# One inference step of a two-layer hybrid trunk on one core: last expert pair's down matrices loaded in column halves, fetched rows of one tile added by the tensor engine, next norm tile by tile inside the pass, roots with scale and bias

## The chip, the core and the metric

The kernel runs on one core of one Trainium2 chip (trn2). The metric is the device time of one execution in microseconds (us), lower is better. The program is written engine by engine: TensorE (PE), VectorE (DVE), ScalarE (ACT), GpSimd (POOL), and the queues that only issue DMAs, SyncE (SP) above all. Each engine runs its own list in order, and waits on semaphores that others raise.

## What is computed

Two layers. Layer 0 mixes tokens with a gated linear recurrence, layer 1 with differential attention; each is followed by a hierarchical mixture of experts. There are 384 tokens (128 context, 256 latent), so three tiles of 128, and a width of 1024. All is float32. Cut to what matters here:

```
def rmsnorm(x, g):
    y = xf * lax.rsqrt(jnp.mean(xf * xf, axis=-1, keepdims=True) + EPS)
    return y * g
def hier_moe(u, ...):            # 4 groups of 4 experts, top-1 group, top-2 experts in it
    h = silu(einsum('nd,edf->nef', xt, w_gate)) * einsum('nd,edf->nef', xt, w_up)
    h = h * combine[:, :, None]                 # two weights per token, else zero
    y = einsum('nef,efd->nd', h, w_down)
# every sub-layer: x = x + gate * f(modulate(rmsnorm(x), shift, scale))
# layer 1 begins with q, k, v = split(modulate(rmsnorm(x)) @ w_qkv, 3)
```

## The kernel before

**The expert stage** (`experts(n)` on each engine, n is the layer) goes over 8 pairs of experts with `expert_passes`: `before`, eight times `body`, then `after`. If an expert had over 64 tokens, further passes would follow in a loop behind `If(count > 1)`; here one pass is enough, and each engine that reaches the end of its first pass loads the count, compares it and jumps over that loop. A pair has six weight matrices of 2 MB (gate and up of two experts, then down of two), which SP loads through a ring of eight slots; `expert_weights` waits until TensorE has used the slot. TensorE gathers the tokens of a pair by a one-hot product (L654), multiplies by gate and up (L665), turns the products (L718) and multiplies by down (`down`, L681) in two column halves of 512, which ACT copies out (L1163, L1166). For seven pairs ACT writes the results into a table in HBM (`expert_rows`).

**The end of the stage.** While the last pair is under way POOL (`collect`, L2023) fetches for every token its two result rows out of that table by six indirect DMAs, two for each tile, into `own` (which lies in `uT`) and into `second_rows` (ring slot 0 in layer 0). DVE (`after`, L1664 to L1669) weights the two rows, adds them and multiplies by the gate; POOL adds the sum to `x` (L2028). Tokens of the last pair do not go through the table: TensorE multiplies its results by the weighted one-hot `wc` (L741, three tiles, two halves), DVE gates that (L1676) and adds it to `x` (L1681), tile by tile, which raises `added`. Ahead of the last `down` TensorE does six products whose result nobody reads (`keep_busy`, L584).

**From layer 0 to layer 1.** ACT squares and sums `x` (L1059) and takes the root (L1063), between the two DVE divides by the width and adds EPS (`mean`, L1385); DVE takes the reciprocal and scales (`normalise`, L1391, L1392), TensorE turns each tile (`turn_tile`, L561, 8 transposes), ACT and DVE each modulate four of its eight feature blocks into `uT` (L1074, L1431), and TensorE starts the projection to q, k, v (L971, 18 blocks of 8 products). Before the turns stand eight more unread products (`keep_busy(8, 512)`). The same chain `square`, `mean`, `root`, `normalise` is used for the second norm of both layers (`second_square`, `second_norm`), for the head norm (`head_mean`, `head_root`), and for q and k in the projection.

**SP's order** at this place: the last pair's six matrices, then the six 2 MB blocks of `attn_w_qkv`, the first one (slot 1) as soon as the pair before last has used that slot.

## Time and profile before

| | |
|---|---|
| median of 3 runs | 1240.55 us (1237.82 to 1240.55) |
| profiled execution, its own time | 1240.84 us |
| its span, first to last instruction | 1239.0 us |
| busy: PE / DVE / ACT / POOL | 1141.3 / 428.6 / 225.6 / 136.1 us |
| DMA, mean over the span | 256 GB/s, 317 MB in all |
| mean granted TensorE clock | 0.976 of full |

The span is cut into 40 slices on the profile's page, with the busy share of each engine, the granted clock and the DMA rate. The timeline gives instructions in order of time, runs of the same kind merged: start, duration, engine, line, output<-inputs, count, and in brackets the idle time before and what ended it. A product of two float32 operands shows as two records, so "x12" is six products. POOL's row for an indirect DMA is the issue alone.

### The profile page before, as it was taken

The page shows a single profiled execution, that of the slowest core. Times are in us where ns is not written, and L with a number is a line of the kernel's source. Part 1 is how long each engine was busy: PE and PEld are TensorE (multiplying, and loading weights), DVE is VectorE, ACT ScalarE, POOL GpSimd, SP SyncE. Part 2 cuts the span into 40 slices and gives each one's busy share as a digit, 9 for nine tenths or more (in the row PEclk, how much of TensorE's full clock was granted, in tenths as well). Part 3 has the DMA queues.
Part 4 walks back from the last instruction along what each step waited for, and adds up shares of the span by engine and source line. Part 5 has one row for each costly group of instructions (what it writes and reads, how often), then busy time and mean ns, then how long its engine had stood idle before and what let it go on. Part 6 is the DMA issues. An engine that isn't in the chain of part 4 may idle for free.

```text
span 1239.0 us, 20044 instructions
## 1 busy us (share of the span) xinstructions
PE 1141.3 (92%) x8612; PEld 681.9 (55%) x8612; DVE 428.6 (35%) x1108; ACT 225.6 (18%) x523; POOL 136.1 (11%) x219
## 2 busy tenths in 40 slices
PE   4999999998899999999989899998989899999885
PEld 2566666665444576666654444444545756666552
DVE  2155555555522350100003755307853420000007
ACT  2210101011111321011000311116632221011010
POOL 0343433333100000000002100000000000000012
PEclk9999999999899999999989899998999999999998
DMA  9973444434923348999999913226751279999993
GB/s 337 316 242 110 138 138 137 137 137 176 380 103 125 136 163 335 424 426 426 424 426 409 346 68 115 106 100 237 262 235 64 73 295 426 426 425 426 424 423 143
DMA packets 97601, 317.08 MB, mean 256 GB/s; under 512 B 3792, under 2 KB 38912, under 8 KB 81120
## 3 DMA queue, kind: packets, MB, share of 16 engines
q1 hardware_dynamic: 90160, 298.05, 62.8%
q10 hardware_dynamic: 5248, 10.97, 2.3%
q0 software_dynamic: 2096, 6.67, 1.5%
q8 instruction: 72, 1.18, 0.4%
q14 instruction: 25, 0.20, 0.1%
HBM read 304.67 MB, written 11.01 MB: 255 GB/s over the span
## 4 chain that ended last, share of the span: by engine, by line
issue 70%; PE 20%; DVE 3%; DMA 3%; POOL 1%; ACT 0%; POOLq 0%; DVEq 0%
PE bank L775 10%; PE bank L784 4%; DMA ring<-expert_rows,moe_row 2%; PE bank L800 2%; PE bank L470 1%; DVE ring L1666 1%; DMA ring<-in_w_ada 1%; PE bank L856 1%; PE bank L809 0%; DVE hg_kf L1759 0%; PE bank L849 0%; DVE uT L1664 0%; PE bank L867 0%; PE bank L476 0%; DVE uT L1676 0%
## 5 line engine op out<-in xcount | busy, mean ns | idle before, releaser
L665 PE MATMUL bank<-ring,xn 128*64 128x256 f32 x1536 | 175.4, 387 | 10.7 <-DMA ring<-in_moe_w_up 7.9
L665 PEld LDWEIGHTS bank<-ring,xn 128*64 128x64 f32 x1536 | 112.1, 140 | 76.5 <-issue 12.8
L775 PE MATMUL bank<-uT,ring 128*128 128x384 f32 x384 | 135.0, 496 | 0.9 <-DVE uT L1712 0.9
L971 PE MATMUL bank<-ring,uT 128*128 128x512 f32 x288 | 126.6, 595 | 1.3 <-issue 1.3
L1654 DVE TENSOR_TENSOR moe_hh<-xn,bank 128x256 f32<-128x256 f32 x32 | 13.5, 421 | 308.0 <-ACT xn L1151 307.9
L2019 POOL TENSOR_TENSOR moe_flag<-con 128x1 f32<-128x1 f32 x2 | 0.4, 192 | 850.8 <-DMA expert_rows<-xn 850.8
L654 PE MATMUL bank<-moe_g,moe_h 128*128 128x128 f32 x768 | 92.2, 277 | 0.4 <-DVE moe_g L1552 0.4
L775 PEld LDWEIGHTS bank<-uT,ring 128*128 128x128 f32 x384 | 69.2, 190 | 42.1 <-issue 2.0
L654 PEld LDWEIGHTS bank<-moe_g,moe_h 128*128 128x128 f32 x768 | 88.2, 192 | 6.1 <-issue 6.1
L971 PEld LDWEIGHTS bank<-ring,uT 128*128 128x128 f32 x288 | 53.9, 191 | 65.4 <-issue 65.4
L681 PE MATMUL bank<-ring,xn 128*64 128x512 f32 x384 | 85.0, 595 | 0.6 <-DMA ring<-in_moe_w_down 0.6
L575 PE MATMUL bank<-ring,uT 128*128 128x512 f32 x192 | 84.0, 592 | 0.0
L1720 DVE COPY_PREDICATED hg_att<-masks,bank 128x384 f32<-128x384 uint8 x104 | 59.9, 576 | 0.0
L575 PEld LDWEIGHTS bank<-ring,uT 128*128 128x128 f32 x192 | 35.9, 190 | 42.2 <-issue 42.1
L665 PE MATMUL bank<-moe_ring,xn 128*64 128x256 f32 x512 | 57.2, 380 | 1.3 <-DMA moe_ring<-in_moe_w_up 1.3
L470 PE MATMUL bank<-ring,cT 128*32 128x512 f32 x384 | 53.8, 684 | 3.8 <-DMA ring<-in_w_ada 3.8
L681 PEld LDWEIGHTS bank<-ring,xn 128*64 128x64 f32 x384 | 27.4, 137 | 50.6 <-issue 49.5
L1151 ACT ACTIVATE xn<-bank 128x256 f32<-128x256 f32 x32 | 12.3, 383 | 206.4 <-PE bank L665 206.4
L665 PEld LDWEIGHTS bank<-moe_ring,xn 128*64 128x64 f32 x512 | 37.4, 137 | 22.1 <-issue 3.9
L784 PE MATMUL bank<-ring,uT 128*128 128x128 f32 x384 | 47.2, 277 | 0.0
L784 PEld LDWEIGHTS bank<-ring,uT 128*128 128x128 f32 x384 | 44.7, 192 | 0.6
L904 PE MATMUL bank<-ring,uT 128*128 128x512 f32 x96 | 42.2, 594 | 0.6 <-DVE adaln L1404 0.5
(269 smaller groups left out, 1306.2 us busy)
## 6 DMA issues: line engine op xcount, KB each, us to landing
ring<-in_w_ada SPq DMA_DIRECT2D x24, 2048.0 KB, 9.9
ring<-in_moe_w_gate SPq DMA_DIRECT2D x24, 2048.0 KB, 18.2
ring<-in_moe_w_up SPq DMA_DIRECT2D x24, 2048.0 KB, 22.4
ring<-in_moe_w_down SPq DMA_DIRECT2D x24, 2048.0 KB, 27.5
ring<-in_hgrn_w_in SPq DMA_DIRECT2D x32, 512.0 KB, 8.3
moe_ring<-in_moe_w_gate SPq DMA_DIRECT2D x8, 2048.0 KB, 22.5
moe_ring<-in_moe_w_up SPq DMA_DIRECT2D x8, 2048.0 KB, 24.1
moe_ring<-in_moe_w_down SPq DMA_DIRECT2D x8, 2048.0 KB, 21.1
```

The lines of the kernel that those rows point to most:

```text
L470: last = mm(bank[to][32 * g:32 * g + 32, :], cT[:, 2 * g + r, :], cols(slot)[:, 2 * g + r, :], start=(r == 0), stop=(r == 1))
L575: last = mm(bank[4 + half][:, :], uT[:, k, t * P:(t + 1) * P], cols(slot)[:, k, :], start=(k == 0), stop=(k == KC - 1))
L654: last = mm(bank[half][:, k * P:(k + 1) * P], m["h"][:, t, (4 * half + k) * P:(4 * half + k + 1) * P], m["g"][:, t, :, :], start=(t == 0), ...
L665: last = mm(bank[2 + e][64 * g:64 * g + 64, 256 * part:256 * part + 256], m["xe"][:, k, 64 * e:64 * e + 64], cols(slot)[:, k, 256 * g:256 ...
L681: last = mm(bank[5 + 2 * half][64 * e:64 * e + 64, :], m["hT"][:, e, j, 64 * g:64 * g + 64], rows_of[e][:, g, j, 512 * half:512 * half + 512],
L775: last = mm(to[:, 0:TOK], w[:, k, f, :], uT[:, k, :], start=(k == 0), stop=(k == KC - 1))
L784: last = mm(bank[3][:, t * P:(t + 1) * P], uT[:, k, t * P:(t + 1) * P], w[:, k, 1, :], start=(k == 0), stop=(k == KC - 1))
L800: last = mm(to[g * size:(g + 1) * size, here], lhs[:, here], rhs[:, here], start=True, stop=True)
L904: last = mm(bank[4 + half][:, :], uT[:, k, t * P:(t + 1) * P], cols(2 + half)[:, k, :], start=(k == 0), stop=(k == KC - 1))
L971: last = mm(bank[b % 2][:, :], uT[:, k, t * P:(t + 1) * P], cols(slot)[:, k, :], start=(k == 0), stop=(k == KC - 1))
L1654: v.tensor_tensor(m["hh"][:, e, :], m["sg"][:, e, :], bank[2 + e][:, 256:512], ALU.mult)\
L1720: return v.copy_predicated(HG["att"][:, :].rearrange("p (t n) -> p t n", t=T), mask, src[:, 0:TOK].rearrange("p (t n) -> p t n", t=T))
```

## The change

1. Last pair: the two down matrices are loaded as four DMAs of 512 columns each (`last_down`), first the left halves of both experts, then the right halves. The k order in the slot becomes (k p), and the turns of the last pair (L718 before) take adjacent columns to match. TensorE waits for the left halves alone (`down_half`), after two unread products instead of six.
2. TensorE's order for the last pair: down left half, the last pair's share of all three tiles for the left half (`first_halves`), down right half, the right half of tiles 0, 2 and 1, and then, for tile 1, four products by a diagonal of weights (`rw`, built by DVE from `ident`) that add its fetched rows in PSUM.
3. DVE's `after`: tile 0 complete, then the fetched rows of tile 2, then the norm of tile 0, tiles 1 and 2 in halves, norms of 1 and 2. POOL's three adds are gone.
4. Layer 0 alone: ACT squares and takes the roots inside the pass (`after` on ACT); TensorE turns tile 0 directly, without the eight unread products, and tiles 1 and 2 in the middle of the first two projection blocks. ACT modulates all of tile 0.
5. `mean` goes everywhere: the root takes scale 1/n and a bias column `eps`. `root_table` loads the root's table ahead at three places.
6. SP loads the first `attn_w_qkv` block when the last fetched rows have landed (`rows2`) instead of when slot 1 is free; the block of slot 0 waits for ACT's last root.

The core of the diff:

```
+                    if last:
+                        for part in range(4):
+                            expert_weights(n, i, part, p)
+                        last_down(n, p)
+                        return
...
+                for half in range(2):
+                    here = slice(512 * half, 512 * half + 512)
+                    for e in range(2):
...
+                        src = a["moe_w_down"][n, 2 * (PAIRS - 1) + e].rearrange("(k p) n -> p k n", p=P)
+                        sp.dma_start(down_rows(slot).rearrange("p g j n -> p (g j) n")[:, :, here], src[:, :, here])\
+                            .then_inc(S[n]["down_half"] if half == 0 else full[n][slot], 16)
...
-                sp.wait_ge(used[0][slot], count * USES + uses_before[0][slot])
-                if slot == SLOT_ORDER[0][0]:
-                    sp.wait_ge(S[0]["added"], count * T + (T - 1))
+                if b == 0:
+                    sp.wait_ge(S[0]["rows2"], count * 32)
...
-                        keep_busy(6, 512)
-                    rows_of = [down_rows(weights_in(i, 4 + e)) for e in range(2)]
+                        keep_busy(2, 512)
+                        pe.wait_ge(s["down_half"], at_pass[0] * 32 + 32)
...
+                        if half == 1 and i == PAIRS - 1:
+                            first_halves(it)
...
+                    last_pair(0, 1, True, True).then_inc(s["last_mm"], 1)
+                    last_pair(2, 1, True, True).then_inc(s["last_mm"], 1)
+                    last_pair(1, 1, True, False)
+                    pe.wait_ge(s["rows1"], p * 32 + 32)
+                    fetched_rows(0)
+                    fetched_rows(1).then_inc(s["last_mm"], 1)
...
-            keep_busy(8, 512)
-            for t, banks in enumerate(((6, 4), (2, 3), (5, 7))):
-                need(pe, 1, "xn_ready", t + 1)
-                turn_tile(1, "xT_done", xn, t, banks)
+            turn_features(0)
...
+                        if b < 2 and k == (6, 4)[b]:
+                            turn_features(b + 1)
...
+                    if n == 0:
+                        root_table()
+                        for t in range(T):
+                            act.wait_ge(s["added"], p * T + (T + t))
+                            A(second_rows[n][:, t, :], x[:, t, :], ACT.Square, accum_out=stat[:, 0, t:t + 1])\
+                                .then_inc(norm_act, 1)
+                            act.wait_ge(norm_act, p * (2 * T) + (2 * t + 1))
+                            root_of(stat[:, 2, t:t + 1], stat[:, 0, t:t + 1], D).then_inc(norm_act, 1)
...
+                    rows_summed(0)
+                    gated_rows(0)
+                    last_added(0, 0)
+                    last_added(0, 1)
+                    rows_summed(2)
+                    if n == 0:
+                        next_norm(0)
+                    for t in range(1, T):
+                        last_added(t, 0)
+                        last_added(t, 1)
+                    if n == 0:
+                        next_norm(1)
+                        next_norm(2)
...
-                    for t in range(T):
-                        pool.wait_ge(s["placed"], p * PLACED + (LAST_WEIGHTED + 3 * t + 3))
-                        g.tensor_tensor(x[:, t, :], x[:, t, :], second_rows[n][:, t, :], ALU.add).then_inc(s["row_added"], 1)
```

How TensorE's list reads from the turns of the last pair to the end of the pass, before (con is the constant tile of the unread products, moe_wc the weighted one-hot):

```order
L718 MATMUL bank<-con,moe_hh 128x128 x4
L584 MATMUL bank<-con 128x512 x6
L681 MATMUL bank<-ring,xn 64x512 x16
L741 MATMUL bank<-xn,moe_wc 128x512 x6
```

and with the change:

```order
L772 MATMUL bank<-con,moe_hh 128x128 x4
L609 MATMUL bank<-con 128x512 x2
L713 MATMUL bank<-ring,xn 64x512 x8
L724 MATMUL bank<-xn,moe_wc 128x512 x3
L713 MATMUL bank<-ring,xn 64x512 x8
L724 MATMUL bank<-xn,moe_wc 128x512 x3
L739 MATMUL bank<-uT,moe_rw 128x512
L739 MATMUL bank<-ring,moe_rw 128x512
L739 MATMUL bank<-uT,moe_rw 128x512
L739 MATMUL bank<-ring,moe_rw 128x512
```

Three of the six products of L741 moved between the halves of down; four products of L739 are new, at the end.

ACT's list from the last root to the first block of the projection, in the first pass of the change (L1241 is the square, L1122 the root; this is the end of the pass):

```order
L1241 ACTIVATE ring,stat<-x 128x1024
L1122 ACTIVATE stat<-stat,con 128x1
L334 TENSOR_LOAD npass
L334 ISA x2
L349 COMPARE_AND_BRANCH
L350 UNCONDITIONAL_BRANCH
```

and what it jumps to (L1137 modulates, L1371 is the first square of the projection):

```order
L1137 ACTIVATE uT<-bank,mod 128x128 x12
L1358 REGISTER_ALU
L1359 DMA at_v<-in_cache_v 128x1024
L1371 ACTIVATE xn<-bank 128x512
```

Before, the pass ended with L1166, and the squares and roots stood behind the jump. Now all three squares and roots stand ahead of it, and every modulation of tile 0, which the first projection block waits for, behind it.

TensorE's list where layer 1 begins, with the change (L586 turns a tile, L1028 is the projection, L1010 turns heads); before it was eight unread products, 24 turns, then 16 projection products without a break:

```order
L586 MATMUL bank<-con,xn 128x128 x8
L1028 MATMUL bank<-ring,uT 128x512 x7
L998 REGISTER_ALU
L586 MATMUL bank<-con,xn 128x128 x8
L1028 MATMUL bank<-ring,uT 128x512 x6
L998 REGISTER_ALU
L586 MATMUL bank<-con,xn 128x128 x8
L1028 MATMUL bank<-ring,uT 128x512 x3
L1010 MATMUL bank<-con,xn 128x128 x4
```

The turns of tiles 1 and 2 now stand inside the first two blocks.

## Rows read from the trace of the kernel before

**Rows 1.** Page, slices of 31 us, and busy time by engine in one stretch:

```profile
GB/s 337 316 242 110 138 138 137 137 137 176 380 103 125 136 163 335 424 426 426 424 426 409 346 68 115 106 100 237 262 235 64 73 295 426 426 425 426 424 423 143
480.00:560.00 80.00, 80.00 (x634) 51.58 (x632) 6.41 (x18) 9.14 (x18) 0.00 (x0) 1.00 1.01 425
...
L971 PE MATMUL bank<-ring,uT 128*128 128x512 f32 x288 | 126.6, 595 | 1.3 <-issue 1.3
```

**Rows 2.** DMA by queue (packets, MB, share), windows 672:675, 681:684 and 1200:1203:

```profile
q0 software_dynamic: 211, 0.77, 65.7%
q1 hardware_dynamic: 211, 0.43, 37.9%
...
DMA packets 568, 1.17 MB, mean 390 GB/s; under 512 B 7, under 2 KB 7, under 8 KB 566
...
DMA packets 170, 1.29 MB, mean 429 GB/s; under 512 B 13, under 2 KB 13, under 8 KB 13
```

**Rows 3.** Timeline of layer 0's last pair, PE and ACT:

```profile
659.11 3.67 PE L665 MATMUL bank<-ring,xn 128*64 128x256 f32 x32 [0.20 <-DMA ring<-in_moe_w_up]
...
665.23 5.42 PE L584 MATMUL bank<-con 128*128 128x512 f32 x12 [0.69 <-ACT xn L1157]
...
670.96 7.09 PE L681 MATMUL bank<-ring,xn 128*64 128x512 f32 x32 [0.32 <-DMA ring<-in_moe_w_down]
...
678.90 5.39 PE L741 MATMUL bank<-xn,moe_wc 128*128 128x512 f32 x12 [0.85 <-ACT xn L1166]
```

**Rows 4.** The same timeline, DVE's fetched rows, gates and adds:

```profile
672.09 0.75 DVE L1664 TENSOR_SCALAR uT<-uT,moe_hw 128x1024 f32<-128x1024 f32 x1 [8.35 <-DMA ring<-expert_rows,moe_row]
672.88 1.28 DVE L1666 SCALAR_TENSOR_TENSOR ring<-ring,moe_hw,uT 128x1024 f32<-128x1024 f32 x1
...
681.68 3.25 DVE L1666 SCALAR_TENSOR_TENSOR ring<-ring,moe_hw,uT 128x1024 f32<-128x1024 f32 x1
...
686.11 1.28 DVE L1676 TENSOR_TENSOR uT<-bank,gates 128x512 f32<-128x512 f32 x2
...
693.40 1.23 DVE L1681 TENSOR_TENSOR x<-x,uT 128x1024 f32<-128x1024 f32 x1
```

**Rows 5.** The same timeline, from layer 0's last product to the projection:

```profile
686.12 7.13 PE L584 MATMUL bank<-con 128*128 128x512 f32 x16 [1.84 <-issue]
...
692.20 1.06 ACT L1059 ACTIVATE moe_h<-x 128x1024 f32<-128x1024 f32 x1 [1.31 <-DVE x L1681]
...
694.89 0.17 DVE L1412 COPY mod<-adaln 128x16 f32<-128x16 f32 x1 [0.26 <-issue]
...
696.48 5.38 PE L561 MATMUL bank<-con,xn 128*128 128x128 f32 x24 [3.22 <-DVE xn L1392]
...
697.69 3.15 ACT L1074 ACTIVATE uT<-bank,mod 128x128 f32<-128x128 f32 x8
...
701.65 2.67 PE L971 MATMUL bank<-ring,uT 128*128 128x512 f32 x5
```

**Rows 6.** Windows: PE, PEld, DVE, ACT, POOL busy, granted clock, DMA share, GB/s:

```profile
696.00:702.00 6.00, 5.52 (x25) 5.51 (x26) 5.05 (x15) 4.74 (x14) 0.00 (x0) 0.50 1.05 391
702.00:704.00 2.00, 2.00 (x5) 0.76 (x4) 1.81 (x7) 0.55 (x2) 0.00 (x0) 0.91 1.06 389
...
1207.00:1211.00 4.00, 4.00 (x7) 1.53 (x6) 0.00 (x0) 0.00 (x0) 0.48 (x1) 0.57 1.02 409
```

**Rows 7.** Timeline of layer 1's last pair and the end:

```profile
1206.62 7.11 PE L584 MATMUL bank<-con 128*128 128x512 f32 x12 [0.69 <-ACT xn L1157]
...
1213.66 7.09 PE L681 MATMUL bank<-ring,xn 128*64 128x512 f32 x32
...
1233.61 1.22 DVE L1681 TENSOR_TENSOR x<-x,uT 128x1024 f32<-128x1024 f32 x1
```

**Rows 8.** Timeline of the second norm of tile 2 in layer 0:

```profile
426.90 0.15 DVE L1385 TENSOR_SCALAR stat<-stat 128x1 f32<-128x1 f32 x1 [1.21 <-ACT xn L1059]
...
428.33 1.09 PE L561 MATMUL bank<-con,xn 128*128 128x128 f32 x8 [0.96 <-DVE xn L1392]
```

More of the change, by code:

```diff
@@ L395, in expert_weights @@
                     sp.wait_ge(*free)
+                    if i == 0 and part == 0 and not isinstance(p, int):
+                        if n == 0:
+                            sp.wait_ge(norm_act, p * (2 * T))
+                        else:
+                            sp.wait_ge(S[n]["added"], p * T + (T - 1))
                 elif n == 0:
@@ L1669, in after @@
[L1669 to L1681 removed]
+                        await_step(step(v.tensor_scalar(own_row, own_row, m["hw"][:, 0, t:t + 1], None, ALU.mult)))
@@ L1693, in _ @@
             own(v.tensor_copy(bias_col[:, :], bank[4][:, 32:128]))
-            for t in range(T):
-                mean(0, "squares", "mean_ready", t)
             for t in range(T):
```

235 lines of the change are left out of this document (135 added, 100 removed).

## The prediction

> **What bounds the kernel now.** I read the page's slices first. In the expert stages the DMA rate stands at 424 to 426 GB/s, and TensorE is busy for all of 480 to 560 us [rows 1]: weights and products go side by side, and the DMA sets the pace. Nothing in the change touches that part. It touches the seams: the end of both expert stages, and the start of layer 1. So I read the timeline there. In layer 0 the last gate and up product waits for its matrix until 659.11, the unread products start at 665.23, and down waits for its matrices until 670.96; 7.09 us of down, a copy and 5.39 us of L741 end at 684.3 [rows 3]. From there the chain is DVE's and ACT's: gates and adds from 686.11 to 694.63 [rows 4], then square, root, scale, turns and modulation until the projection starts at 701.65 [rows 5]. The projection itself is TensorE's own: 126.6 us busy, 1.3 us idle [rows 1]. In layer 1 the unread products start at 1206.62, down at 1213.66, and DVE's last add ends at 1234.83; the output and the end of the span, 1239.0, follow 4.2 us behind [rows 7].
>
> **The last down matrices, layer 0.** The four new DMAs carry the same 4.19 MB. Three things change. (a) Packets. A row of 512 float32 is 2 KB, as in the projection's blocks, which run at 390 GB/s where the wide ones run at 429 [rows 2]. (b) The fetched rows compete. While both queues are at work, queue 0 (the rows) and queue 1 move equal numbers of packets, 211 each in 3 us, so queue 1 with its 2 KB packets gets 0.43 MB (143 GB/s) and the rows with 4 KB packets 0.77 MB (257 GB/s) [rows 2]. Wide packets had the better of that; narrow ones do not. (c) The first projection block no longer stands behind them.
> Estimate: the down bytes begin at about 656 (3 us ahead of the landing at 659.11, rows 3) and the rows reach the DMA engines at 665.3. Until then 9.3 x 0.386 MB, less 0.25 MB of other writes, is 3.35 MB; the last 0.84 MB at 143 GB/s take 5.9 us, and with 3 us to the semaphore they land at 674.2. The left halves land before 665.
> TensorE: two unread products, 5.42/6 each, from 665.23 to 667.0; the left half of down (7.09/2) to 670.6; 0.85 for the copy; three products of 0.90 (5.39/6) to 674.1; the right half, just landed, to 677.7; a copy again to 678.5; three products and the four new ones, 6.3 us, to 684.8 [rows 3]. Before, the end was 684.3. The down product starts 4 us earlier and nothing is won: four new products (3.6 us) and a second wait for the copy (0.85) take it.
> A rule of the Trainium skill speaks against this edit: DMA: Bandwidth & Descriptors, section Bandwidth, wants DMAs of 1 MiB and more and measures 341 GB/s at that size against 425 at 16 MB. No row here shows a 1 MB load of this kind by itself; by that rate the estimate for the landing would be 3 us later in each layer.
>
> **DVE after it.** Gone are POOL's three adds, beside which a 1.28 us operation took 3.25 [rows 4]. Tile 0 is gated, added and normed while TensorE works, so it costs nothing as long as that cover holds (it needs the rows by about 679; the first ones landed at 672.09, rows 4). Behind the last product, at 684.8, stand two gate-add pairs for tile 1 and two triples for tile 2: ten half-tile operations at 0.64 (L1676, half of 1.28) plus the gap, say 0.70 each: 691.8, against 694.63. That is 2.8 us won.
>
> **From x to the projection.** ACT's square, read and root of tile 2 cost 1.06 + 0.19 + 0.2, to 693.4. Now what the lists show: ACT's modulation of tile 0 stands behind all three squares and the jump out of the pass. Tile 0 is turned at 688, and nobody modulates it until tile 2's root is out. The jump: TensorE's shows 1.84 us before the next instruction, DVE's 0.26, hidden under a long add [rows 5]. ACT's root takes 0.2 and hides little, so I take 1.3, ends 0.3 and 1.9. Four modulations (half of 3.15) follow [rows 5]: the projection starts at 696.3, 5.3 us earlier.
> Then what is given back. The clock: before, TensorE was idle for 3.2 us, and 696 to 702 ran at 0.50, that is 1.2 GHz instead of 2.4 [rows 5, 6]; it came back about 5.9 us after work resumed, 0.7 us into the projection, and the low stretch had fallen on 24 short turns. Now the eight unread products are gone, TensorE idles from 688 to 696.3, and the low stretch falls on full products: 5.7 us at half speed lose 2.85, against 0.35. The turns of tiles 1 and 2 move into the projection: 16 at full clock, 1.09 per 8 [rows 8], 2.1 us, and 0.4 of waiting for their modulation. So the saving is 5.3 - 2.5 - 2.1 - 0.4 = **0.3 us**, ends -3 (a landing late by 3 us) and +4 (no jump to pay, the clock back early).
> The projection's blocks: the first is requested at about 677.5 and there by 686; the others take 5.4 us each and are needed every 21. Free. The 12 steps of `mean` taken out of the projection's chain are worth 0: TensorE covers them. If that cover were gone, 12 x 0.2.
>
> **The end, layer 1.** The unread products start at 1206.62, and the clock was low from 1207 to 1211 [rows 6, 7]. Two of them and the left half therefore end at about 1213.8, the copy at 1214.6, three products at 1217.3; the right halves, by the working above 2 us slower than before the change, land at about 1216.5. Right half to 1220.9, copy, seven products: 1228.0. Ten DVE operations: 1235.0 to 1235.4, against 1234.83. The output behind it is the same. Cost: **0.4 us**, ends -1.5 and +4.
>
> **Roots.** In the second norm of tile 2 TensorE waits for the chain, 0.96 us, and `mean` is 0.19 of it (from 426.90 to the root) [rows 8]: 0.2 us in each layer, **0.4 us** saved. With the expert stage bound by DMA it is kept only since SP's loads wait for slots that TensorE frees. The table loads are moved from places where they wait beside TensorE's work: 0, save 0.1 at the head norm of layer 1, which its own table load ahead gives back. The first norm of layer 0 lies under the wait for `w_ada`: 0.
>
> **Sum.** -0.3 + 0.4 - 0.4 = -0.3 us on the profiled time of 1240.84, that is 1240.5; the median of the runs lies 0.3 below that execution, so 1240.3.
>
> **The rivals.**
> *Forecast: an even exchange.* 1240.3 within 0.3% (3.7 us, about what a measurement of this kernel tells from no change). Chance 0.58.
> *Faster: the projection's early start is kept.* TensorE's clock does not stay low for long once full products come (4.4 us after work resumed in layer 1, rows 6, 7), ACT pays no jump, and the end of layer 1 gains from landing early. 1.5 (clock) + 1.0 (jump) + 1.5 (layer 1) + 1 (turns hidden in gaps): 1235.5. For it: the jump of DVE at 0.26. Against: an idle time of 3.2 us was enough to lower the clock before, and now it is 8. Chance 0.26.
> *Slower: the right halves land late.* The one mechanism is the equal split by packets: whatever of the 2.1 MB of right halves is still to come when the fetched rows start goes at 143 GB/s. The point of decision is a landing behind 674.1 in layer 0 and 1217.3 in layer 1, from there each us counts once in each layer. If all of the right halves were left, they would take 14.7 us and land about 7 us late. Likely is 3 us in each layer, 1246.5. For it: the split is measured. Against: most bytes should be through by 665. Chance 0.13. The rule on DMA size above would give this result too.
> *It does not do what it says.* The left halves are not early, because four DMAs on the same 16 engines finish together: then TensorE waits until 671 for its left half and ends 4 us late, 1244.5 to 1248. Chance 0.03.
>
> **How the numbers follow.** Faster by over 3.7 us: 0.26. Within: 0.58. Slower: 0.16. The range 1235.5 to 1245.5 takes in the forecast with its ends, most of the faster case and the milder half of the slower one.
>
> **What would show it.** Down's left half starting near 667 and 1209, its right half near 674 and 1217; the last product by `rw` ending near 684.8; DVE's last add of layer 0 near 692; ACT's first modulation 1 to 2 us behind the last root; the first projection product near 696, with a granted clock of 0.5 in the 5 us after it. I am wrong if the right half of down waits for its DMA, if the clock is full when the projection starts, or if anything between 705 and 1200 changes its length.

## The result, and the profile after

| | before | after |
|---|---|---|
| median, runs on the same chip | 1239.02 us (9 runs) | 1245.56 us (9 runs) |
| ratio | | 1.0054, 95% interval 1.0040 to 1.0068 |
| profiled execution / its span | 1240.84 / 1239.0 us | 1247.2 / 1245.4 us |
| busy PE / DVE / ACT / POOL | 1141.3 / 428.6 / 225.6 / 136.1 us | 1129.4 / 412.2 / 230.0 / 120.4 us |

The change makes the kernel 6.5 us slower. The forecast was an exchange, 1240.3 us; the measured time lies just above the range, and it is the time of the rival on the slower side, "the right halves land late" (1246.5 us). TensorE, DVE and POOL are less busy than before (ACT 4 us more): the loss is waiting.

TensorE's timeline of the changed kernel, end of layer 0 and start of layer 1, which answers to [rows 3] and [rows 5] (start us, duration, engine, line, output<-inputs, count, idle time before):

```profile
655.79 3.67 PE L690 MATMUL bank<-ring,xn 128*64 128x256 f32 x32 [1.34 <-DMA ring<-in_moe_w_up]
...
661.82 1.98 PE L609 MATMUL bank<-con 128*128 128x512 f32 x4 [0.69 <-ACT xn L1221]
663.74 3.65 PE L713 MATMUL bank<-ring,xn 128*64 128x512 f32 x16
668.18 2.81 PE L724 MATMUL bank<-xn,moe_wc 128*128 128x512 f32 x6 [0.79 <-ACT xn L1227]
674.22 6.55 PE L713 MATMUL bank<-ring,xn 128*64 128x512 f32 x16 [3.23 <-DMA ring<-in_moe_w_down]
681.54 2.84 PE L724 MATMUL bank<-xn,moe_wc 128*128 128x512 f32 x6 [0.77 <-ACT xn L1230]
...
686.80 1.02 PE L739 MATMUL bank<-ring,moe_rw 128*128 128x512 f32 x2
688.91 1.09 PE L586 MATMUL bank<-con,xn 128*128 128x128 f32 x8 [1.09 <-issue]
698.87 8.79 PE L1028 MATMUL bank<-ring,uT 128*128 128x512 f32 x14 [8.87 <-ACT uT L1137]
```

L713 is down, L724 the last pair's share, L739 the products by `rw`, L1028 the projection. The left half starts at 663.74 without a wait, 8.0 us behind the start of the last up product (655.79); before, down started 11.9 us behind it. Then the right half waits 3.23 us for its DMA, and takes 6.55 us where the left one took 3.65. The last product ends at 687.8, 32.0 us behind that same point; before, it was 25.2 [rows 3].

The DMA queues of the changed kernel in three stretches of 3 us (packets, MB, share of the 16 engines' time), first 661 to 664:

```profile
q0 software_dynamic: 207, 0.78, 66.5%
q1 hardware_dynamic: 207, 0.41, 36.1%
```

667 to 670:

```profile
q0 software_dynamic: 268, 0.99, 83.5%
q1 hardware_dynamic: 113, 0.22, 19.0%
```

670 to 673:

```profile
q0 software_dynamic: 139, 0.48, 39.6%
q1 hardware_dynamic: 41, 0.08, 6.7%
```

Queue 0 carries the fetched rows, queue 1 the right halves. At first they move equal numbers of packets, 207 each, as in [rows 2]. Later queue 1 gets less than half, and at the end 41 packets in 3 us: both queues together move 0.56 MB there (187 GB/s), and TensorE waits. Queue 1's last packets move between 673 and 674.

The granted clock of the changed kernel in those stretches (columns: stretch, length, busy PE, PEld, DVE, ACT, POOL, clock, DMA share, GB/s):

```profile
672.00:676.00 4.00, 1.78 (x6) 0.64 (x8) 0.93 (x2) 0.00 (x0) 0.00 (x0) 0.66 0.29 70
676.00:680.00 4.00, 4.00 (x12) 1.27 (x10) 0.00 (x0) 0.00 (x0) 0.00 (x0) 0.50 1.04 402
680.00:684.00 4.00, 3.23 (x10) 1.25 (x7) 1.26 (x2) 2.08 (x3) 0.00 (x0) 0.99 1.06 389
...
700.00:704.00 4.00, 4.00 (x6) 1.55 (x5) 0.00 (x0) 0.13 (x1) 0.00 (x0) 0.50 1.05 385
704.00:708.00 4.00, 4.00 (x14) 1.97 (x13) 0.00 (x0) 0.00 (x0) 0.00 (x0) 1.00 0.99 365
```

While TensorE waits for the right half the clock falls to 0.50 of full, that is 1.2 GHz for 2.4, and the right half is multiplied at that. It falls again in the 8.87 us without work before the projection, and comes back behind 704.

DVE's timeline of the changed kernel, which answers to [rows 4]:

```profile
666.92 0.75 DVE L1748 TENSOR_SCALAR uT<-uT,moe_hw 128x1024 f32<-128x1024 f32 x1 [6.50 <-DMA ring<-expert_rows,moe_row]
...
682.71 0.69 DVE L1765 TENSOR_TENSOR ring<-bank,gates 128x512 f32<-128x512 f32 x1 [9.74 <-PE bank L724]
...
687.86 0.69 DVE L1765 TENSOR_TENSOR ring<-bank,gates 128x512 f32<-128x512 f32 x1 [0.76 <-PE bank L739]
...
694.01 0.69 DVE L1766 TENSOR_TENSOR x<-x,ring 128x512 f32<-128x512 f32 x1
```

And ACT's, behind the last addition:

```profile
694.74 1.06 ACT L1241 ACTIVATE ring<-x 128x1024 f32<-128x1024 f32 x1 [2.62 <-DVE x L1766]
...
695.92 0.29 ACT L1122 ACTIVATE stat<-stat,con 128x1 f32<-128x1 f32 x1
697.22 2.90 ACT L1137 ACTIVATE uT<-bank,mod 128x128 f32<-128x128 f32 x8 [1.01 <-issue]
```

DVE waits 9.74 us for TensorE in the middle, and 6.8 us of additions follow the last product. ACT starts the modulation of tile 0 only at 697.22, 1.01 us behind the last root.

The end of layer 1, TensorE and then DVE, which answers to [rows 7]:

```profile
1203.74 3.67 PE L690 MATMUL bank<-moe_ring,xn 128*64 128x256 f32 x32 [1.67 <-DMA moe_ring<-in_moe_w_up]
...
1211.69 3.65 PE L713 MATMUL bank<-ring,xn 128*64 128x512 f32 x16
...
1222.07 5.35 PE L713 MATMUL bank<-ring,xn 128*64 128x512 f32 x16 [3.12 <-DMA ring<-in_moe_w_down]
```

```profile
1234.55 0.69 DVE L1765 TENSOR_TENSOR ring<-bank,gates 128x512 f32<-128x512 f32 x1 [1.82 <-PE bank L739]
...
1240.71 0.69 DVE L1766 TENSOR_TENSOR x<-x,ring 128x512 f32<-128x512 f32 x1
```

The right half waits 3.12 us here too. From the start of the last up product to the end of DVE's last addition it is 37.7 us; before 34.7.

To see where time goes, I cut each trace at seven points: the first gate product of layer 0, the last up product of layer 0, the projection's first product, the first scores of the attention, the same two points in layer 1, and DVE's last addition. The stretches from gate to last up product are 212.8 to 213.1 us long in both layers of every trace but one, where the last up product of layer 0 shows no gap of its own. The others (us, from start to start; the last column runs to the end of the addition):

| trace | start to first gate product | last up to projection | projection to scores | scores to layer 1's experts | last up, layer 1, to last addition |
|---|---|---|---|---|---|
| before | 446.0 | 42.5 | 134.4 | 151.1 | 34.7 |
| after | 442.8 | 43.1 | 139.0 | 152.9 | 37.7 |
| before, second trace | 444.6 | (255.8 from the first gate product; before 255.6) | 134.4 | 151.1 | 34.7 |
| after, second trace | 446.1 | 41.7 | 138.3 | 150.3 | 36.0 |
| rows held | 442.6 | 36.9 | 138.7 | 153.6 | 32.8 |
| gap filled | 444.3 | 40.2 | 139.1 | 151.3 | 36.0 |
| projection filled (8) | 444.5 | 41.7 | 138.2 | 152.7 | 37.6 |
| whole matrices | 443.9 | 44.1 | 138.8 | 152.6 | 39.3 |
| no products by rw | 444.9 | 41.0 | 139.0 | 152.9 | 36.0 |
| held and filled | 443.4 | 38.5 | 136.4 | 153.6 | 32.8 |
| the same, whole matrices | 443.4 | 40.9 | 136.4 | 151.7 | 34.8 |
| the same, order swapped | 445.3 | 36.9 | 136.5 | 152.7 | 31.0 |
| the same, turn outside | 445.1 | 40.5 | 134.9 | 151.7 | 32.8 |
| the last two together | 444.3 | 40.5 | 134.9 | 150.3 | 31.0 |

The first and the fourth column differ by 3.3 and 2.6 us between the two traces of the changed kernel alone, so they say nothing of an edit of a few us. In the fourth it goes with the clock: what the granted clock lacked of full, summed over slices of 5 us, is 5.1 us in the two traces of 150.3 us, 6.8 in the four of 151.1 to 151.7 (the kernel before twice among them), 8.5 to 8.6 in the five of 151.7 to 152.9, and 10.2 to 10.3 in the three of 152.6 to 153.6. The other three columns are what the experiments are read by. (Rows held is experiment 1 below, gap filled 2, projection filled 3, whole matrices 4, held and filled 6, no products by rw 7, and the last four rows are 8 to 11.)

### The profile page after: what moved, and what is told of

Same layout as the page of the kernel before. It is cut to its first block, busy times and chain, and to the rows that moved or that the text cites. A ratio compares the mean times of both kernels' runs of the same rounds, so it can differ in the third digit from the quotient of the medians.

```text
span 1245.4 us, 19994 instructions
## 1 busy us (share of the span) xinstructions
PE 1129.4 (91%) x8596; PEld 673.9 (54%) x8596; DVE 412.2 (33%) x1087; ACT 230.0 (18%) x530; POOL 120.4 (10%) x213
## 4 chain that ended last, share of the span: by engine, by line
PE 73%; DMA 12%; DVE 5%; ACT 2%; SPq 2%; issue 2%; ACTq 0%; DVEq 0%
PE bank L690 13%; PE bank L1028 10%; PE bank L829 10%; PE bank L600 7%; PE bank L713 7%; DMA ring<-in_moe_w_up 6%; PE bank L679 5%; DMA ring<-in_moe_w_down 5%; PE bank L838 4%; PE bank L958 3%; PE bank L495 3%; SPq L428 2%; DMA ring<-in_w_ada 2%; PE bank L854 2%; PE bank L579 1%
## 5 line engine op out<-in xcount | busy, mean ns | idle before, releaser
L690 PE MATMUL bank<-ring,xn 128*64 128x256 f32 x1536 | 172.6, 383 | 10.2 <-DMA ring<-in_moe_w_up 7.4
L1028 PE MATMUL bank<-ring,uT 128*128 128x512 f32 x288 | 129.5, 604 | 10.5 <-ACT uT L1137 9.2
L713 PE MATMUL bank<-ring,xn 128*64 128x512 f32 x384 | 90.1, 622 | 8.5 <-DMA ring<-in_moe_w_down 8.5
L1028 PEld LDWEIGHTS bank<-ring,uT 128*128 128x128 f32 x288 | 54.3, 193 | 75.5 <-issue 74.4
L600 PE MATMUL bank<-ring,uT 128*128 128x512 f32 x192 | 84.0, 593 | 0.0
L713 PEld LDWEIGHTS bank<-ring,xn 128*64 128x64 f32 x384 | 28.8, 142 | 61.8 <-issue 60.8
L495 PE MATMUL bank<-ring,cT 128*32 128x512 f32 x384 | 51.0, 653 | 5.8 <-DMA ring<-in_w_ada 5.8
L1215 ACT ACTIVATE xn<-bank 128x256 f32<-128x256 f32 x32 | 12.3, 384 | 204.4 <-PE bank L690 196.2
L958 PE MATMUL bank<-ring,uT 128*128 128x512 f32 x96 | 42.2, 594 | 0.6 <-DVE adaln L1473 0.5
```

The lines of the kernel that those rows point to most:

```text
L495: last = mm(bank[to][32 * g:32 * g + 32, :], cT[:, 2 * g + r, :], cols(slot)[:, 2 * g + r, :], start=(r == 0), stop=(r == 1))
L600: last = mm(bank[4 + half][:, :], uT[:, k, t * P:(t + 1) * P], cols(slot)[:, k, :], start=(k == 0), stop=(k == KC - 1))
L690: last = mm(bank[2 + e][64 * g:64 * g + 64, 256 * part:256 * part + 256], m["xe"][:, k, 64 * e:64 * e + 64], cols(slot)[:, k, 256 * g:256 ...
L713: last = mm(bank[5 + 2 * half][64 * e:64 * e + 64, :], m["hT"][:, e, j, 64 * g:64 * g + 64], rows_of[e][:, g, j, 512 * half:512 * half + 512],
L958: last = mm(bank[4 + half][:, :], uT[:, k, t * P:(t + 1) * P], cols(2 + half)[:, k, :], start=(k == 0), stop=(k == KC - 1))
L1028: last = mm(bank[b % 2][:, :], uT[:, k, t * P:(t + 1) * P], cols(slot)[:, k, :], start=(k == 0), stop=(k == KC - 1))
```

## The experiments

Three theories were weighed. A: the right halves share the DMA engines with the fetched rows and land late, and the wait lowers the clock. B: the order itself costs, with its four products by `rw` and its second copy, whenever the data lands. C: the loss is in layer 1's start, from clock, turns and ACT's order. The first four ran together on one chip (kernel before: 1237.77 us), the next four on another occasion (1238.02), the last four on a third (1238.21); each ratio is to the kernel before beside it.

**1. Hold the fetched rows back until the left halves have landed.**

```
@@ collect, POOL
+                    pool.wait_ge(s["down_half"], p * 32 + 32)
                     g.tensor_tensor(m["flag"][:, 1:2], ones[:, 0:1], ones[:, 0:1], ALU.mult)
```

> The changed kernel with one wait more: POOL starts the fetch of rows only when the left halves of the last down matrices have landed. Theory A (the fetched rows on queue 0 and the right halves on queue 1 share the DMA engines packet by packet, the right halves land 3.2 us late in layer 0 and 3.1 us late in layer 1, and each wait lowers TensorE's clock): the right half of down starts without a DMA wait in both layers, takes 3.7 us in place of 6.55 and 5.35, and the last product ends about 5.5 us earlier in layer 0 and 4.5 us earlier in layer 1. Of the 5.5 in layer 0 about 1 us can be lost where the rows now land later than the products by them want them. Total 8 to 10 us less than the changed kernel: 1235 to 1238. Theory B (the four products by the fetched rows, the second copy and the order of products cost the time, whenever the halves land): under 3 us less, 1243 or more. Theory C (the loss lies in layer 1's start, clock and turns inside the projection): the gain of layer 0 is kept as far as DVE's adds follow the products.

Measured: 1237.59 us, ratio 1.0004 (0.9987 to 1.0021). TensorE's timeline:

```profile
655.61 3.67 PE L690 MATMUL bank<-ring,xn 128*64 128x256 f32 x32 [1.22 <-DMA ring<-in_moe_w_up]
...
667.99 2.81 PE L724 MATMUL bank<-xn,moe_wc 128*128 128x512 f32 x6 [0.79 <-ACT xn L1227]
670.74 3.65 PE L713 MATMUL bank<-ring,xn 128*64 128x512 f32 x16
...
680.43 1.02 PE L739 MATMUL bank<-ring,moe_rw 128*128 128x512 f32 x2
...
692.49 8.52 PE L1028 MATMUL bank<-ring,uT 128*128 128x512 f32 x14 [9.57 <-ACT uT L1137]
```

Queues of this kernel, 660 to 663, 663 to 666, 666 to 669:

```profile
q1 hardware_dynamic: 545, 1.08, 97.5%
```

```profile
q0 software_dynamic: 59, 0.24, 32.9%
q1 hardware_dynamic: 142, 0.27, 23.1%
```

```profile
q0 software_dynamic: 257, 0.95, 91.8%
```

Alone, queue 1 moves its 2 KB packets at 387 GB/s (586 packets, 1.16 MB, from 657 to 660) and at 360 in the next 3 us, and is through by 666, before TensorE asks at 670.7. The right half waits for nothing and takes 3.65 us. The projection starts 6.2 us earlier after the last up product than in the changed kernel, the last addition of layer 1 4.9 us earlier. The rows arrive 2.9 us later than in the changed kernel (DVE's first operation on them at 669.66 in place of 666.92, with nearly the same up product), and nobody waits for them behind that. Theory A holds, and B falls as the main cause: the same order of products, without the late landing, is even with the kernel before. The three stretches of this one trace add up to 3.3 us less than before, while the medians are even and the interval allows 1.6 us less. In its fourth column it is 2.5 us longer than the kernel before; how much of the gain in the stretches an average execution keeps stays open.

**2. Keep TensorE busy while the right half is awaited.**

```
@@ down, TensorE
                             first_halves(it)
+                            fill(1, 3)
                             for e in range(2):
                                 weights_in(i, 4 + e)
```

(`fill(to, times)` is `keep_busy` with the bank as an argument.)

> The changed kernel with three unread products of 512 columns (0.95 us each) between the three products of the left half and the wait for the right half, into a bank that nobody reads. Theory A with the clock as a cost of its own: the right halves land as late as before, but TensorE stays at full clock, so the right half takes 3.7 us in place of 6.55 in layer 0 and 5.35 in layer 1: 3 to 4.5 us less than the changed kernel, 1241 to 1242.5. If the low clock after the wait has another cause, or if the time is given back behind it, nothing: 1245.5.

Measured: 1243.29 us, ratio 1.0046 (1.0028 to 1.0063).

```profile
672.29 2.74 PE L614 MATMUL bank<-con 128*128 128x512 f32 x6
675.68 3.65 PE L719 MATMUL bank<-ring,xn 128*64 128x512 f32 x16 [0.65 <-DMA ring<-in_moe_w_down]
```

The landing stays where it was, 18.4 and 18.3 us behind the last up product, but the clock holds and the right half takes 3.65 us in both layers. So the wait and the clock are two costs: 3.2 us and up to 2.9 us in layer 0, 3.1 and up to 1.7 in layer 1. (The 2.9 stands in one trace. In the three other traces with a late landing and nothing in the gap the clock cost 1.5 to 1.7 us, but nothing in layer 1 of the second trace in experiment 5.) By the ratios the clock's part is 1 to 3.6 us, against the two runs of the changed kernel (1.0054, and 1.0075 in experiment 5); the three intervals overlap, so it rests on the trace.

**3. Keep TensorE busy before the projection, eight products.**

```
@@ before the projection, TensorE
             turn_features(0)
+            fill(1, 8)
```

> The changed kernel with eight unread products of 512 columns (0.95 us each, 7.6 us) between the turn of tile 0 and the projection of layer 1, where TensorE is idle for 8.9 us. Theory C: the first 14 records of the projection take 6.2 us in place of 8.79 and the attention stage starts 2.6 us earlier: 1243. If the fill runs past the first modulation (it starts 7 to 8 us behind the turn), up to 1 us of it is lost. If ACT or the turns pace the first blocks, nothing: 1245.5.

Measured: 1243.51 us, ratio 1.0043 (1.0024 to 1.0061).

```profile
690.04 7.03 PE L614 MATMUL bank<-con 128*128 128x512 f32 x16
699.13 7.94 PE L1034 MATMUL bank<-ring,uT 128*128 128x512 f32 x14 [2.06 <-ACT uT L1143]
```

A miss: the 14 records take 7.94 us, not 6.2. The fill ended 2.06 us before the first modulated blocks were there, and the clock fell again: 0.86 from 698 to 700, 0.50 from 700 to 702. How long such a gap may be is not shown: in experiment 9 the fill ended 1.59 us early and in experiment 10 TensorE was idle for 2.32 us between its unread products, and the clock stayed at 1.00 in both. What the cost is had to be asked once more, in experiment 6.

**4. Undo the column halves, with the k order and the turns that belong to them.**

```
@@ SP, last pair
-                        for part in range(4):
-                            expert_weights(n, i, part, p)
-                        last_down(n, p)
+                        for part in range(len(PARTS)):
+                            expert_weights(n, i, part, p)
                         return
@@ down, TensorE
-                        pe.wait_ge(s["down_half"], at_pass[0] * 32 + 32)
+                        rows_of = [down_rows(weights_in(i, 4 + e)) for e in range(2)]
...
```

> The changed kernel with the column halves alone undone: the last pair's down matrices come whole, in 4 KB packets, with the turns that belong to them, and the left half of down waits for both; everything behind it (the three products in the middle, the products by the fetched rows, the norm in the pass, the roots) stays. Theory A: wide packets hold their share beside the fetched rows, the matrices land 12 us behind the last up matrix (as before the change), the left half starts 4 us later than in the changed kernel, the right half does not wait and runs at full clock: the last product ends 2 to 3 us earlier in each layer, 1240 to 1242. Theory B: both halves of down start later and the extra products still follow, so the end is 2 us later than in the changed kernel in each layer: 1248 to 1250.

Measured: 1249.26 us, ratio 1.0092 (1.0064 to 1.0119).

```profile
656.85 3.67 PE L689 MATMUL bank<-ring,xn 128*64 128x256 f32 x32 [1.18 <-DMA ring<-in_moe_w_up]
...
669.12 6.52 PE L709 MATMUL bank<-ring,xn 128*64 128x512 f32 x16 [4.18 <-DMA ring<-in_moe_w_down]
```

Each theory had half of it. The whole matrices land 12.3 us behind the last up product (13.1 in layer 1), near the 11.9 of the kernel before [rows 3]. Their packets are 8 KB, and not 4 KB as the expectation says (160 packets, 1.29 MB, from 655 to 658): the column halves cut them to a quarter. With nearly equal numbers of packets from 661 to 664, 114 and 90, queue 1 moves 0.88 MB beside 0.37 MB of rows, where the halves got 0.41 beside 0.78. So wide packets hold their own beside the fetched rows, though not for nothing: with the rows held they land at 10.0 (experiment 8). But my sum from that was wrong: the time is B's number. With two unread products in place of six TensorE is idle for 4.18 us, its clock falls, the left half takes 6.52 us, and the middle products, the second copy and the products by `rw` follow one after another: the last product ends 33.0 us behind the last up product, where it was 25.2 before. So B's work is a cost where the data comes late, and the halves, even late, are worth 2 to 5 us against whole matrices in this order.

**5. The changed kernel, and the kernel before, again.** No edit.

> The changed kernel once more, unaltered, as the yardstick of the three beside it on this chip and as a second trace of its seams. All theories: ratio 1.0054 to the kernel before, within 0.0015; by the trace, 43.1 us from the last up matrix of layer 0 to the projection, 139.0 on to the attention stage, 37.7 from the last up matrix of layer 1 to DVE's last add, with a right half that waits 3.1 to 3.2 us in each layer and takes 5.2 to 6.6 us after it, by where the clock falls.

> The kernel before once more, unaltered, for a second trace. What is open: its profiled execution reached the expert stage of layer 0 at 446.0 us where five executions of the changed kernel and its variants reached it at 442.6 to 444.5, with a clock of 0.66 from 320 to 330 us that the changed kernel's trace does not have. If that is the chance of one execution, this trace reaches it at 443 to 444; if the change took it out (the means and roots), at 446 again. From the last up matrix of layer 0 on both theories expect the same as before: 42.5, 134.4, and 34.7 us at the end of layer 1.

Measured: 1246.26 us, ratio 1.0075 (1.0057 to 1.0092), for the changed kernel; one execution of the kernel before took 1239.52. The first gate product came at 444.6 in the kernel before and at 446.1 in the changed one: the 3.2 us between the first two traces lie within what executions of one kernel differ by, and are no sign of a gain by the roots. In the second trace of the changed kernel the right halves land at 18.41 and 18.34 us behind the last up product, where the first has 18.43 and 18.33. What moves between executions is the clock. In layer 1 of the second trace:

```profile
1209.40 3.60 PE L609 MATMUL bank<-con 128*128 128x512 f32 x4 [0.69 <-ACT xn L1221]
...
1220.67 3.65 PE L713 MATMUL bank<-ring,xn 128*64 128x512 f32 x16 [0.46 <-DMA ring<-in_moe_w_down]
```

Here it fell earlier, under the unread products (3.60 us for two in place of 1.98), the wait shrank to 0.46 us and the right half ran at full clock.

**6. Hold the rows, and fill with ten products before the projection.**

```
@@ collect, POOL
+                    pool.wait_ge(s["down_half"], p * 32 + 32)
@@ before the projection, TensorE
             turn_features(0)
+            fill(1, 10)
```

> The changed kernel with the fetch held back until the left halves have landed (as in the first of these runs) and ten unread products (8.8 us) in the 9.6 us that TensorE is idle between the turn of tile 0 and the projection. Theory C with enough fill to hold the clock: the projection's first 14 records take 6.3 to 6.6 us in place of 8.5, and the stretch from the projection to the attention stage falls from 138.7 to 136.5: 2 us below the held kernel, which puts it 2 us below the kernel before, ratio 0.9985. If the turns inside the projection and ACT's modulation pace the first blocks, the clock is worth under 1 us, as eight products were (138.15 against 138.97).

Measured: 1234.61 us, ratio 0.9964 (0.9951 to 0.9978): faster than both kernels.

```profile
686.08 8.75 PE L614 MATMUL bank<-con 128*128 128x512 f32 x20
694.96 6.25 PE L1034 MATMUL bank<-ring,uT 128*128 128x512 f32 x14
```

With the fill up to the last moment the clock holds at 1.00 throughout, and 14 records take 6.25 us: 2.3 us less than in the held kernel (8.52), 2.5 less than in the changed one (8.79). That is what the low clock costs at the start of the projection. The fill itself delays nothing here: the projection starts 1.65 us behind ACT's first modulation, as in the changed kernel. Against the held kernel it is 3 us by the medians and 5 by the ratios, on two occasions; the trace accounts for 2.3. In layer 0 of this trace the clock fell under the two unread products before down (3.36 us in place of 1.98), so the projection starts 38.5 us behind the last up product and not 36.9; in experiment 9, with the same code up to there, it is 36.9.

**7. Give tile 1's rows back to DVE.**

```
@@ first_halves, TensorE
-                    last_pair(1, 0, True, False)
+                    last_pair(1, 0, True, True)
...
@@ after, TensorE
-                    last_pair(1, 1, True, False)
-                    pe.wait_ge(s["rows1"], p * 32 + 32)
-                    fetched_rows(0)
-                    fetched_rows(1).then_inc(s["last_mm"], 1)
+                    last_pair(1, 1, True, True).then_inc(s["last_mm"], 1)
@@ after, DVE
                     last_added(0, 0)
+                    rows_summed(1)
+                    gated_rows(1)
                     last_added(0, 1)
```

> The changed kernel with one part alone undone: tile 1's two fetched rows are scaled, added and gated by DVE (four operations, 4.5 us) while it waits for the right half's products, and the four products by rw are gone. Theory B (those four products, 3.5 us at the end of TensorE's work, are what the layer pays): DVE's last add comes 3.4 us earlier in each layer, 1238.5 to 1239. Theory A (with right halves this late DVE itself is the bound: the four operations fit into its 9.7 us of waiting, but the two of tile 2 and the norm of tile 0 then stand in front of tile 1): the last product ends 3.5 us earlier and DVE's last add 0.5 to 1.5 us: 1243 to 1245.

Measured: 1244.24 us, ratio 1.0051 (1.0038 to 1.0064), beside 1.0075 for the changed kernel on the same chip. In the trace DVE does the four operations between 674.67 and 679.27, inside its wait, and from 683.63 on works without a gap to 694.8. From the last up product to the projection it takes 0.7 us less than in the second trace of the changed kernel (right half 5.35 and 5.17 us), and the end of layer 1 1.7 us less than in the first (right half 5.35 us in both). By the medians it is 2.0 us in all, by the ratios 3.0, with intervals that overlap. So the products by `rw` are some 2 to 3 of the 8 to 9 us lost on this chip while the right halves are late; in the held kernel, where DVE's wait in the middle is 0.63 us instead of 9.74, they are what keeps 4.6 us of work off DVE. That last was not tried.

**8. Held and filled, with whole matrices.** The edit of experiment 4 on the kernel of experiment 6, and POOL waits for the first of the two matrices.

> The held and filled kernel with the column halves undone: the last down matrices come whole in 4 KB packets, the left half of down waits for both, and the fetch is held until the first of the two has landed. It tells what the halves themselves are worth once the fetched rows no longer collide with them. By the held trace the left half starts 8 us behind the last up matrix; two whole matrices end about 10 to 11 us behind it, so the left half starts 2 to 3 us later, the right half runs without a wait, and each layer ends 2 to 3 us later: 4 to 6 us over the held and filled kernel, 1239 to 1240.5. If it is the same as the held and filled kernel, the halves were worth nothing and the gain was the hold and the fill alone.

Measured: 1239.02 us, ratio 1.0007 (0.9994 to 1.0020).

```profile
666.31 5.61 PE L714 MATMUL bank<-ring,xn 128*64 128x512 f32 x16 [1.03 <-DMA ring<-in_moe_w_down]
```

The left half waits 1.03 us and starts 10.0 us behind the last up product. In experiment 6 it was 9.3, in experiment 1, where the unread products ran at full clock, 7.9. Each layer ends 2.0 to 2.3 us later than in experiment 6, and the medians differ by 4.4 us (the ratios by 5.3, on two occasions): that is what the column halves are worth once nothing collides with them.

**9. Swap DVE's last additions in layer 1.** On the kernel of experiment 6.

```
@@ after, DVE
-                    for t in range(1, T):
+                    for t in ((1, 2), (2, 1))[n]:
@@ outputs, SP
-            for t in range(T):
-                sp.wait_ge(S[1]["added"], count * T + t)
+            for i, t in enumerate((0, 2, 1)):
+                sp.wait_ge(S[1]["added"], count * T + i)
```

> The held and filled kernel with DVE's last additions in layer 1 in the order tile 2, tile 1, and the output DMAs in that order: in the trace DVE stands idle for 1.82 us before tile 1's products by rw are done, while tile 2's products have been there for 3 us. From the last up matrix to DVE's last add 32.8 us become 31.1, the total 1.6 us less than the held and filled kernel. If the output behind the last add then waits for the two earlier outputs, some of it is lost there: 4.0 us from the last add to the end of the span would grow.

Measured: 1233.34 us, ratio 0.9957 (0.9940 to 0.9974). DVE's timeline:

```profile
1220.23 1.28 DVE L1755 SCALAR_TENSOR_TENSOR ring<-ring,moe_hw,uT 128x1024 f32<-128x1024 f32 x1
1221.55 0.69 DVE L1769 TENSOR_TENSOR ring<-ring,bank 128x512 f32<-128x512 f32 x1
...
1227.70 0.69 DVE L1772 TENSOR_TENSOR x<-x,ring 128x512 f32<-128x512 f32 x1
```

The gap before the additions is gone, the stretch is 31.0 us for 32.8, and 4.0 us still follow it. The gain of the trace is 1.8 us; the medians give 1.3 and the ratios 0.9, which is within their intervals. This is the fastest version by the ratio, though its interval overlaps with those of experiments 6 and 11. Before the projection the fill ended 1.59 us early, and the 14 records still took 6.25 us:

```profile
695.10 6.25 PE L1034 MATMUL bank<-ring,uT 128*128 128x512 f32 x14 [1.59 <-ACT uT L1143]
```

**10. Tile 1's turn outside the projection.** On the kernel of experiment 6: four unread products, the turn of tile 1, five more, and ACT modulates all of tile 1.

> The held and filled kernel with tile 1's turn taken out of the projection and put into the time in which TensorE is idle before it (four and five unread products around it in place of ten), tile 1's second modulation done by ACT in place of DVE so that the order of the two stays fixed, tile 2's turn left where it is. Theory C (a turn inside the projection costs its 1.04 us, and only that): the stretch from the projection to the attention stage falls from 136.4 to 135.4, total 1.0 us less than the held and filled kernel. If ACT, with four more modulations (1.45 us), delays the projection's second block, nothing or up to 0.5 us more.

Measured: 1235.58 us, ratio 0.9977 (0.9965 to 0.9990).

```profile
693.35 1.09 PE L586 MATMUL bank<-con,xn 128*128 128x128 f32 x8 [2.32 <-DVE xn L1785]
694.28 4.46 PE L614 MATMUL bank<-con 128*128 128x512 f32 x10
698.58 11.32 PE L1036 MATMUL bank<-ring,uT 128*128 128x512 f32 x26
```

A miss by my placing. The stretch from the projection to the scores does fall by 1.5 us, to 134.9. But DVE scales tile 1 only behind the additions of tile 2, so the turn waits until 693.35, and the five unread products behind it hold up the projection until 698.58, 2.0 us later than in experiment 6. The turn's price is a little more than theory C's 1.04 us: with it goes the 0.30 us for which the second block waited. The fill was too long by the 2.0 us, since ACT's first modulation came 36.9 us behind the last up product, as in experiment 6.

**11. Experiments 9 and 10 together.**

> The last two edits together on the held and filled kernel: additive, 2.6 us less than the held and filled kernel, near 1232, ratio to the kernel before 0.9945.

Measured: 1233.69 us, ratio 0.9973 (0.9959 to 0.9988). The trace adds up as its two parts do (40.5, 134.9 and 31.0 us in the three stretches), with the same 2 us lost in front of the projection. Its ratio is not better than that of experiment 9. A fill of two or three products behind the turn was not tried.

## Why the prediction was wrong, point by point

**The landing of the right halves: the step that failed.** I put it 15.1 us behind the last up product in layer 0 (674.2 against 659.11) and 16.3 in layer 1; in the five traces with a late landing it was 18.3 to 18.4 in both. The mechanism was in the text, the equal split by packets, and 207 packets each in 3 us show it. The size was off in three terms. The rows reached the engines 5 us behind the last up product, not 6.2, so 1.1 MB instead of 0.84 was still to come; by my own rate and delay that alone makes 15.7. The large one is the rate. Queue 1 did not keep 143 GB/s, and the 1.1 MB took about 12.5 us in place of 7.7: from 667 on it moved 0.22 MB in 3 us (73 GB/s), then 0.08 (27 GB/s), with 6.7% of the engines' time at the end. That is little more than one of the 16 engines (6.25%), so the last packets seem to wait in a few engines' share of the work; no view shows single engines, and this stays open. The third term went the other way: of the 3 us from the last bytes to the semaphore at most 1.2 are there, since the last packets move between 673 and 674 and TensorE starts at 674.22. The rival's "point of decision" was rightly placed, and in layer 0 my own landing, 674.2, stood 0.1 us on its far side. An estimate that ends exactly on the edge of a rival is a coin toss for it, not 0.13. The rival's worst case was also added up wrongly: 665.3 + 14.7 + 3 is 683, 9 us behind 674.1 and not 7.

**The clock after the wait: missing.** I had the clock in the projection, but not behind a late right half. Experiment 2 shows it: up to 2.9 us in layer 0 and 1.7 in layer 1 (1.5 to 1.7 in most traces), on top of 3.2 and 3.1 of waiting. The rival's "3 us in each layer" was the wait alone.

**TensorE's work in between: right.** Unread products, left half, copy and three products were to take 8.9 us from the start of the unread ones to the request for the right half; the trace has 9.2 (661.82 to 671.0). The copy and the last seven products: 7.1 foreseen, 7.1 measured (680.77 to 687.8).

**DVE and ACT behind it: right.** Seven us of additions (6.8), 1.45 us of square and root (1.5), a jump of 1.3 us (1.01), 1.6 us of modulation (1.65). ACT's modulation of tile 0 does stand behind all squares and the jump.

**What is given back: right.** The clock in the projection was to cost 2.85 us; it costs 2.5 (8.79 against 6.25). The turns were to cost 2.1 and a wait of 0.4; from the projection to the scores it is 136.4 us with the clock held, against 134.4 before, so 2.0 with the wait, or 2.4 without the 0.35 us of low clock that I counted in the kernel before. So the net of -0.3 us in layer 0 would have held, and come out at -1.4, with the landing on time: in the held kernel the last up product is followed by the projection 5.7 us sooner than before (36.9 against 42.5; I had 5.3), and 4.3 us are given back (138.7 against 134.4; I had 5.0).

**Layer 1: wrong by the same step.** 0.4 us foreseen, 3.0 and 1.3 us in the two traces. I also carried the low clock of [rows 6] over to the changed kernel; it falls where the execution puts it. Without the late landing the stretch is 32.8 us, 1.9 better than before, and better than my lower end of -1.5. But little of that need be the change's: in both traces of the kernel before the six unread products of layer 1 took 7.11 us, against 5.42 at full clock in layer 0, and in the held kernel's trace the clock did not fall there.

**Roots: 0.4 us, not confirmed and not refuted.** The start to the first gate product varies by 3.5 us between executions. TensorE's wait for tile 2 in the second norm of layer 0 went from 0.96 to 0.90 and 0.87 us in the two traces, where I had expected 0.2 less.

**The sum.** By the stretches the first trace has 0.5 + 4.5 + 3.0 - 0.2 = 7.9 us over the kernel before, the second -0.9 + 3.9 + 1.3 - 0.2 = 4.1; the medians say 6.5 and 8.2.

**The rule on DMA size.** The Trainium skill, DMA: Bandwidth & Descriptors, section Bandwidth, gives 341 GB/s for 1 MB. My estimate from that figure was a landing 3 us later, and the landing was 3.3 us later in layer 0 and 2.0 in layer 1. That is a match by luck, for the runs do not bear out this cause: the halves alone move at 387 GB/s (1.16 MB from 657 to 660 in the held kernel), and with the rows out of the way they are there in time.

## What to carry to other kernels

Splitting a load so that its first part comes early only pays if nothing slips in front of the second part: look at which transfers are released in that time, and hold the one that is needed later. Hold a transfer back by the landing of the other and not by a guess; here one wait on GpSimd was worth 6 to 9 us by the ratios, and 7.6 to 11.4 by the traces. Count the packets as well as the bytes: column halves turned 8 KB packets into 2 KB ones, and beside rows that moved as many packets of up to 4 KB they got 0.41 MB of 1.19. When a change removes unread products, count the clock as a cost of its own wherever TensorE then waits, and read from the trace where the fill ends: eight products ended 2.06 us early and gained 0.1 to 0.8 us in the stretch behind them, ten gained 2.3, and in experiment 10 the fill ended 2 us late.

## What the runs showed that I had not expected

- The equal split by packets does not last to the end of the transfers (rows first, right halves second): 207 and 207 packets at first, then 268 and 113, then 139 and 41, at 187 GB/s for both together at the end. In layer 1 it is milder: 220 and 218 packets from 1211 to 1214, 172 and 120 from 1217 to 1220 (277 GB/s).
- Fetched rows alone move more slowly than the halves alone, 289 to 358 GB/s in three stretches of the held kernel against 387. Per byte the difference is small: 257 packets took 91.8% of the engines' time in 3 us for 0.95 MB, so 0.17 us of one engine for 3.7 KB, where queue 1 takes 0.09 us for 2 KB (586 packets in 3 us).
- The same wait costs differently from one execution to the next: in two traces of the changed kernel the right half took 6.55 and 5.17 us in layer 0, 5.35 and 3.65 in layer 1, by whether the clock had fallen before.
